# A hybrid decoder layer: the mixer in two passes over the tokens, with thirty gather batches of the channel mixer inside the second

## What is computed

```
h  = RMSNorm(x) * (1 + scale1) + shift1
y  = sigmoid(h @ W_gate_a) * (o_mla @ W_mla) + sigmoid(h @ W_gate_b) * (o_dil @ W_dilb)
x += gate1 * (y @ W_out)                       # the mixer's end
h2 = RMSNorm(x) * (1 + scale2) + shift2
# channel mixer (PEER): 8 heads, each picks 16 of 16384 experts
q  = h2 @ w_pq ; s = q . sub_keys              # 8 heads x 2 halves x 128 scores
top 16 of each half -> 256 sums -> top 16 pairs -> eidx, g = softmax
a  = gelu(h2 . expert_u[eidx]) * g
x += gate2 * sum over 8 x 16 picks of a * expert_v[eidx]
```

## Time and profile before

| | us |
|---|---|
| median of 3 runs | 4351.54 |
| lowest and highest | 4319.0, 4370.52 |
| the profiled execution's own time | 4370.86 |
| its span | 4369.1 |
| TensorE busy | 3802.1 (87%) |
| VectorE busy | 2723.7 (62%) |
| ScalarE busy | 1199.4 (27%) |

### The profile page before, as it was taken

How to read it: one execution, slowest core, us unless ns; L and a number is a source line. 1 busy time by engine, 2 the same in 40 slices (tenths; PEclk the granted TensorE clock), 3 DMA queues, 4 the chain that set the end, 5 groups by cost and what they waited for, 6 DMA issues and landing times.

```text
span 4369.1 us, 43255 instructions
## 1 busy us (share of the span) xinstructions
PE 3802.1 (87%) x14474; PEld 2490.1 (57%) x14474; DVE 2723.7 (62%) x6374; ACT 1199.4 (27%) x3244; POOL 859.8 (20%) x718
## 2 busy tenths in 40 slices
PE   8798899999981899967997677799999999899896
PEld 7575377888970788953453444344454444445443
DVE  2764562533534111258999987767779676967876
ACT  2564432322332111122222567421111111111111
POOL 0000000001000000003333223333333333344332
PEclk8898998995985899988999888899999999999997
DMA  4001102203116111237888879999999999999997
GB/s 158 7 1 42 29 37 80 81 20 119 51 40 208 55 41 36 100 108 282 323 327 318 314 302 376 399 417 409 410 399 378 414 412 387 384 409 412 387 354 279
DMA packets 255851, 1016.29 MB, mean 233 GB/s; under 512 B 28650, under 2 KB 103810, under 8 KB 170642
## 3 DMA queue, kind: packets, MB, share of 16 engines
q0 software_dynamic: 101520, 723.10, 41.9%
q1 hardware_dynamic: 131218, 280.65, 17.4%
q10 hardware_dynamic: 22896, 9.80, 0.8%
HBM read 964.22 MB, written 49.25 MB: 232 GB/s over the span
## 4 chain that ended last, share of the span: by engine, by line
PE 27%; DVE 15%; DMA 11%; issue 2%; ACT 2%; SPq 0%; POOL 0%; ACTq 0%; DVEq 0%
PE banks L2488 9%; PE banks L2474 9%; DMA ff_room<-in_v 7%; PE banks L2463 4%; DVE ff_rows L2137 4%; PE banks L2411 2%; DVE ff_acc L2103 2%; DMA gates_dram<-ff_room 2%; PE banks L2356 1%; DMA ff_rows<-in_uv,pk_expert 1%; DVE pk_eq L1793 1%; DVE pk_axes L1798 1%; DVE mx_x L2163 1%; PE banks L2435 1%; DVE pk_besti L1772 1%
## 5 line engine op out<-in xcount | busy, mean ns | idle before, releaser
L2035 POOL DMA_INDIRECT ff_rows<-in_uv,pk_expert x640 | 803.0, 1255 | 1519.2 <-DVE ff_acc L2103 831.8
L2137 DVE CUSTOM_DVE_ANT_0 ff_rows<-ff_rows,ff_h_row 128x1024 f32<-128x1024 f32 x648 | 766.6, 1220 | 45.3 <-DMA ff_rows<-in_uv,pk_expert 43.4
L2488 PE MATMUL banks<-ff_room,mx_x 128*128 128x512 f32 x1536 | 702.3, 608 | 57.9 <-DVE mx_x L2178 31.2
L2474 PE MATMUL banks<-mx_x,ff_room 128*128 128x384 f32 x2048 | 685.7, 488 | 12.2 <-ACT mx_x L2321 12.2
L2463 PE MATMUL banks<-ff_rows,o_mla_tops 128*128 128x512 f32 x904 | 446.5, 643 | 144.5 <-ACT o_mla_tops L2231 140.8
L2474 PEld LDWEIGHTS banks<-mx_x,ff_room 128*128 128x128 f32 x2048 | 390.3, 191 | 313.0 <-issue 77.3
L2488 PEld LDWEIGHTS banks<-ff_room,mx_x 128*128 128x128 f32 x1536 | 297.3, 195 | 418.9 <-issue 357.8
L2103 DVE SCALAR_TENSOR_TENSOR ff_acc<-ff_rows,ff_a,ff_acc 128x1024 f32<-128x1024 f32 x388 | 498.6, 1285 | 7.2
L2463 PEld LDWEIGHTS banks<-ff_rows,o_mla_tops 128*128 128x128 f32 x904 | 179.1, 206 | 361.8 <-issue 198.5
L177 PE MATMUL banks<-d_w_high,h_high 128*128 128x512 f32 (+1 forms) x648 | 274.3, 423 | 21.9 <-DVE d_w_low L184 21.0
L2219 ACT ACTIVATE ff_gelu<-ff_dots 128x2 f32<-128x2 f32 x324 | 65.7, 203 | 824.9 <-DVE ff_dots L2137 824.7
(11 more groups left out here) (391 smaller groups left out, 5660.3 us busy)
## 6 DMA issues: line engine op xcount, KB each, us to landing
ff_room<-in_uT SPq DMA_DIRECT2D x128, 512.0 KB, 14.4
ff_room<-in_v SPq DMA_DIRECT2D x128, 512.0 KB, 20.6
gates_dram<-ff_room SPq DMA_DIRECT2D x6, 4096.0 KB, 16.8
mx_x<-gates_dram SPq DMA_DIRECT2D x128, 192.0 KB, 17.2
d_w<-in_w_dil POOLq DMA_DIRECT2D x9, 2048.0 KB, 8.3
d_w<-in_w_ada POOLq DMA_DIRECT2D x32, 512.0 KB, 4.7
ff_room<-in_w_pq SPq DMA_DIRECT2D x32, 512.0 KB, 4.5
ff_rows<-in_uv,pk_expert POOLq DMA_INDIRECT x640, 10.8
```

The source lines that it names most:

```text
L2035: pool.indirect_dma_start(out=rows[r][:, :], out_offset=None, in_=IN["uv"][:, :], in_offset=bass.IndirectOffsetOnAxis(ap=at, axis=0))\
L2137: ins = dve.tensor_tensor_reduce(rows[r][:, 0:D], rows[r][:, 0:D], h_row[i % 2][:], 1.0, 0.0, ALU.mult, ALU.add, dots[:, B % RB, j:j + 1])
L2474: ins = pe.matmul(SD[:, 0:ND], u[e % 4][:, k, :], hd[:, k, :], start=(k == 0), stop=(k == KD - 1))
L2488: ins = pe.matmul(Y[j][:, half], ad[e % 2][:, j * P:(j + 1) * P], v[e % 4][:, half_rows[half]], start=(e == 0), stop=(e == NK - 1))
```

## The change

The mixer goes over the tokens in two passes: tokens 0 to 255 (the first two tiles) as one column block of 256, gates, output projection and normalisation, and then tokens 256 to 1031 in two blocks of 388. A unit is now one gate with its branch for one block: 16 units in pass 1, 32 in pass 2 (`z` counts them). Weights are loaded once for each pass, one block of 512 KB at a time, in four slots in pass 1 and two in pass 2. The two slots that pass 2 leaves are the ring of two batches (`RB` = 2 in `stage_mix`).

Behind unit 1 of pass 2 (`ROUTER_AT`) stand the router of tiles 0 and 1 and the picks of the first half of tile 0's heads; the rest of tile 0's picks behind units 2 to 4. Then 30 of tile 0's 64 batches (`MIX_BATCHES`) stand behind the units of `BATCH_AT`; the six last ones lie in the output projection. All their sums are VectorE's, into `acc0`. The sums of a batch stand in front of the mixer products of the next unit.

The channel mixer begins with batch 30 of tile 0 as its batch `B` = 0 and has 98 in place of 128 before the dense loop. It has no router in front; the rows of `h` go out through SP's queue, between the weight loads of the late router, from two buffers that are free at the time. VectorE's early sums are now at every third of batches 3 to 30. The tables `PIECES`, `HOT0` (58 for 61) and `HOTS` (three quads a batch for two) are set anew.

```diff
+EARLY, MIX_BATCHES = 2, 30
 def stage_mix(c):
+    CB = (TOK - NE) // 2
+    PASSES = [[(0, NE)], [(NE, NE + CB), (NE + CB, TOK)]]
+    SUBS = [(p, m, side, i) for p in range(2) for m in range(KD) for side in range(2) for i in range(len(PASSES[p]))]
+    NB, RB = MIX_BATCHES, 2
+    ROUTER_AT = 1
+    BATCH_AT = [z for z in range(5, 31) if z not in (16, 28)] + list(range(33, 48, 2))
+    batch_at = {z: b for b, z in enumerate(BATCH_AT[0:NB])}
...
+            @block.gpsimd
+            def _(pool):
+                pool.wait_ge(s["half_tile"], 1)
+                for b in range(NB):
+                    for j in range(G):
+                        r = b % RB * G + j
+                        if b >= RB:
+                            pool.wait_ge(s["rsum"], (b - RB) * G + j + 1)
...
+                def gated(u):
+                    p, m, side, i = SUBS[u]
+                    if u >= 3:
+                        pe.wait_ge(s["y"], u - 2)
+                    for k in range(KO):
+                        pe.matmul(out, wb[b % 2][:, side * KO + k, :], src[:, k, c0:c1], start=(k == 0), stop=(k == KO - 1))
+                    pe.wait_ge(s["w_lo"], n + 1)
+                    for k in range(KD):
+                        ins = product3(pe, gate, w_parts(n, k), [t[:, k, c0:c1] for t in h_parts], k == 0, k == KD - 1)
...
+                def weights(b):
+                    act.wait_ge(s["dot"], b + 1)
+                    act.activation(act_of[:, b % RB], dots[:, b % RB], ACT.Gelu).then_inc(s["gelu"], 1)
+                    act.wait_ge(s["gelu"], b + 1)
+                    for j in range(G):
+                        ins = act.activation(a[:, b % RB, j:j + 1], act_of[:, b % RB, j:j + 1], ACT.Copy,
+                                             scale=c.gate0[:, b * G + j:b * G + j + 1])
+                    ins.then_inc(s["a"], 1)
...
+                def sums_due(z):
+                    if z in batch_at and batch_at[z]:
+                        sums(batch_at[z] - 1)
...
+                for z in range(len(SUBS) - S1):
+                    sums_due(z)
+                    mixed(S1 + z)
+                    for n in made_after(S1 + z):
+                        w_low(dve, n)
+                    if z == ROUTER_AT:
+                        for hp in range(HP):
+                            dve.wait_ge(s["sc_copy"], hp + 1)
+                            for part in range(4):
+                                top16(part, hp)
+                                dve.wait_ge(s["top"], hp * 4 + part + 1)
+                        pk.prepare(dve)
+                        picks(0)
+                        picks(1)
+                    if 2 <= z <= 4:
+                        picks(z)
+                    dots_due(z)
...
 def stage_ffn(c):
-    batches = [(i, b) for i in range(NS) for b in range(TAILB if i == TAIL else PER)]
+    batches = [(i, b) for i in range(NS) for b in range(0 if i else MIX_BATCHES, TAILB if i == TAIL else PER)]
-    PICK0, HOT0, HOTS = HP * LATE_PER + 3, HP * LATE_PER + 13, 2
+    PICK0, HOT0, HOTS = HP * LATE_PER + 3, HP * LATE_PER + 10, 3
-    TURN0 = 112
+    TURN0 = 86
-    PIECES = {4 + 8 * k: (1, k) for k in range(5)}
-    PIECES |= {PICK0 + 10 * j + 2 * k: (t, k) for j, t in enumerate(DENSE) for k in range(5)}
-    PIECES |= {PICK0 + 59 + 3 * k: (2, k) for k in range(5)}
+    PIECES = {2 + 6 * k: (1, k) for k in range(5)}
+    PIECES |= {PICK0 + at + step * k: (t, k) for t, at, step in zip(DENSE, (0, 6, 16), (1, 2, 2)) for k in range(5)}
+    PIECES |= {PICK0 + 29 + 3 * k: (2, k) for k in range(5)}
-    ON_VEC = list(range(LATE_PER, HP * LATE_PER, LATE_PER))
+    ON_VEC = list(range(LATE_PER, first[1] - 1, LATE_PER))
+    transit = [acc[1], h_row[1]]
...
-                for n in range(2 * HP):
+                for n in range(HP):
                     if n >= 2:
                         sp.wait_ge(s["q_mm"], n - 1)
+                    sp.dma_start(w[n % 2], IN["w_pq"][n]).then_inc(w_in[n % 2], 16)
+                    if n == 1:
+                        for i in range(2, NS):
+                            t0, m = TILES[SPARSE[i]]
+                            sp.wait_ge(s["h_copy"], i)
+                            sp.dma_start(c.dram["h_rows"][t0:t0 + m], transit[i % 2][0:m]).then_inc(h_out[i % 2], 16)
...
-                for hp in range(HP):
-                    dve.wait_ge(s["sc_copy"], hp + 1)
-                    for part in range(4):
-                        top16(dve, part, range(EARLY), hp)
-                        dve.wait_ge(s["top"], hp * 4 + part + 1)
```

More of the change, by code:

```diff
@@ L1563, in stage_mix @@
         ts = sb("ts", [P, KD, NSA])
[L1564 to L1568 removed]
+        dots, act_of, a = (sb(t, [P, RB, G]) for t in ("dots", "gelu", "a"))
@@ new lines, in _ @@
+                for n in range(S1, S1 + 4):
+                    weight(n)
+                sp.wait_ge(s["mm"], S1)
+                residual(0)
+                for n in range(S1 + 4, W1):
+                    weight(n)
+                branch(KD)
+                branch(KD + 1)
+                weight(W1)
+                weight(W1 + 1)
+                keep(0)
+                weight(W1 + 2)
+                for n in range(2, HP):
+                    queries(n)
+                weight(W1 + 3)
@@ new lines, in sums @@
+                def sums(b):
+                    dve.wait_ge(s["a"], b + 1)
+                    for j in range(G):
+                        v, weight = ring[:, b % RB * G + j, D:2 * D], a[:, b % RB, j:j + 1]
+                        if b == 0 and j == 0:
+                            ins = dve.tensor_scalar(acc, v, weight, None, ALU.mult)
+                        else:
+                            dve.wait_ge(s["rsum"], b * G + j)
+                            ins = dve.scalar_tensor_tensor(out=acc, in0=v, scalar=weight, in1=acc, op0=ALU.mult, op1=ALU.add)
+                        ins.then_inc(s["rsum"], 1)
```

658 lines of the change are left out of this document (428 added, 230 removed).

## The result

| | before | changed |
|---|---|---|
| median of 16 runs, us | 4364.77 | 4306.22 |
| lowest and highest | 4319.0, 4373.51 | 4296.85, 4322.61 |
| profiled span | 4369.1 | 4300.1 |

The account below looks back on a forecast made before the run. TensorE bounds the mixer, VectorE then mostly the channel mixer, DMA its last stretch and the dense loop. Mixer +87 and channel mixer -155 give -68: 4303 profiled, 4351.5 - 68 = 4284 us timed, range 4222 to 4365.

Parts of the forecast that it names:

- thirty units of pass 2: Mixer behind the router: TensorE needs 205 us, VectorE's path sums to 214, plus a little mutual loss: 218.
- channel mixer to batch 4: Start of the channel mixer to batch 4's dots: 143 us before, router's 77 gone, 58 expected, bounds 45 and 70.
- Prices: Mixer unit costs: split product 0.120 us at 256 columns, 0.176 at 388; pass 2 unit 6.83; VectorE's step 7.2.
- The turn: Switch from pass 2's units to its output projection, put at 3.5 us within that output's 84.
- The 343 us of one-hot rows: Channel mixer batches 58 to 90: VectorE's 305, some 30 of stalls, 8 for ScalarE; bounds 305 and 395.
- The last eight batches: Channel mixer batches 90 to 98: DMA-bound at 418 GB/s, 57 us less what is fetched ahead: 52, bounds 42 and 60.
- The 13 us by which 218 exceeds 205: Pass 2 of the mixer: the only cost claimed for VectorE's 155 us of gathered work.
- Rival 1: Gathers bind in the mixer's two-batch ring: +45 us; with the split product's upper bound 4350, no change; chance 0.17.
- Rival 2: Larger gain: ScalarE's waits fall beside picks (-30), channel mixer's start 45 us (-13), shorter gelu wait: 4235; chance 0.15.
- Rival 3: Slower: TensorE waits for VectorE in pass 2, so its granted clock falls; in-between case 4410; chance 0.11.
- The signs: Expected profile: pass 2 VectorE gaps over 1 us only before sums, TensorE idle 0.4 us a unit, dense loop 1418 us.
- The drain: Skill's 1.38 us beside each ScalarE table load; by it sigmoid comes 0.5 us behind the sums, sum 12 us larger.

Follow-up runs that it names:

- without the stores: Changed kernel with the gates' HBM table filled from expert_v, so ScalarE does not wait for the five stores: total 2826.7 us, ratio 0.9744.
- pieces at the stalls: Changed kernel with sixteen mixer batches, rows of h stored by GpSimd, and pieces of picks placed where VectorE stalled: 2845.9 us, ratio 0.9812; again 2844.0, 0.9823.

## Why the prediction was right, and where it was not

The sign held, and every stage moved the way that was said; which work paid was in part another than the prediction says (below, "What bounds"). Term by term, from the mixer's first matmul:

| term | predicted | measured |
|---|---|---|
| pass 1 with its output | 108 | 114.2 |
| first two units, router | 14 + 77 | 13.7 + 74.6 |
| thirty units of pass 2 | 218 | 222.5 |
| output of pass 2, with the turn | 84 | 90.3 |
| tail | 15 | 15.6 |
| **mixer** | 516 | 531.0 |
| channel mixer to batch 4 | 58 | 54.4 |
| to 48, 58 | 327, 77 | 320.9, 83.0 |
| to 90, 98 | 343, 52 | 345.7, 44.0 |
| **channel mixer** | 857 | 848.0 |

By these terms the change is -62, not -68: 15 too little in the mixer and 9 too much in the channel mixer. That the spans differ by -69.0 all the same is in part luck. The stages ahead gave 3.7 us and the idle time in front of the first matmul 5.0, neither of which had a price, and the end cost 2.0.

- **Prices.** The split product was taken at 0.120 us and measured 0.118, a unit of pass 2 at 6.83 and measured 6.85, VectorE's step at 7.2 and measured 7.27, its wait for the weights at 0.85 and measured 0.78. The slope from 256 to 344 columns carried over to both new widths.
- **The mixer's 15 us.** Pass 1 is 6 longer, since its first unit waits 2.5 for a weight split and then runs at half the clock (granted clock 0.50; 0.21 us a split product up to 1451, then 0.118). The turn was put at 3.5 us and took 7.5: "two engines so near to each other lose a little to one another" was right, but the place was not. The prediction looked for 0.4 us of idle TensorE a unit; from 1692 to 1835 there is none. Beside it 8.2 us of TensorE's wait up to 1684.8 stand behind the picks. A cost that the prediction left out comes behind each of these two waits: from 1685 to 1690 and from 1872.6 to 1876 the granted clock was 0.50, the lower level, and some 18 split products took 0.32 us in place of 0.176, some 2.6 us each time. The thirty units took 221 to 222 us in the runs with two, sixteen and twenty batches as well, so most of their excess over TensorE's 205 is not the batches' doing. Against that, the first matmul comes 5 us nearer to the stage ahead (an idle time of 4.4 for 9.4 us), probably as the first loads are smaller.
- **Channel mixer.** The first late query came 29.0 us behind its start (30 to 35 predicted). The 343 us of one-hot rows, called the weakest term, were 345.7, and for the reason given: 305 of VectorE's work (303) and 38 of stalls and ScalarE (39). The split of those 38 into 30 and 8 was wrong: without the stores 6 us beside VectorE's work are left. The last eight batches were priced at the rate of a full DMA (418 GB/s); they ran at 352 and a share of 0.88 and moved some 15.5 MB, so more was fetched ahead of them than was reckoned.
- **What bounds.** "From 1878 on the channel mixer is bound by VectorE" is the step that misleads, though the sum carried the right numbers. The largest gain beside the router's move, 67 us, came from the last stretch of the earlier trace rows, which the same paragraph called DMA-bound and the sum priced by gathers (111 to 52; measured 111 to 44). The prediction spoke of VectorE's 155 us moved under TensorE; the runs with two, sixteen and thirty batches show that what paid was gathers taken out of a full DMA stretch, and that once that stretch was gone a batch moved, with the closer tables that it needs, cost more than it brought. The 13 us by which 218 exceeds 205 were called the price of VectorE's gathered work; by the runs with fewer batches twenty cost next to nothing and thirty 6 to 10 us, most of it at the end of the mixer.
- **Rival 1**, gathers that bind in the ring of two: no. Its reason "for" (VectorE has no slack) held, its reason "against" (DMA nearly idle) did not, since the gathers themselves bring DMA to 0.88. They landed in 8.2 us (median, 1690 to 1940), and VectorE waited 7.1 us for them in all. **Rival 2**: no; batch 4 came after 54.4 us and not 45, and 40 us of VectorE's waits were left in the one-hot rows. **Rival 3**: the granted clock was 1.00, full speed, from 1692 to 1865, and 0.85 in the 50 us of the picks. What it describes did happen, but only for the few microseconds behind TensorE's two long waits.
- **The signs.** From 1693 to 1870 us VectorE had gaps of over 1 us outside of the place named: three of 2.6 us for a sigmoid, and two for gathers (1.3 and 1.9). The dense loop, from the first to the last matmul of its first kind (L2474), took 1421.0 us for 1418.2.
- **The drain.** The 0.5 us and 12 us that the prediction works out for it are low by its own terms: 2.65 + 1.38 us is 0.6 behind the 3.4, 14 us over 23 units. It changes nothing in the sum.
- **From the trace to the median.** The 4284 us are 22 under the measured 4306. -68 was right for the pair of profiles; the base was not. The three runs shown had a median of 4351.5, sixteen have 4364.8, and from that the same sum gives 4297. The "19.3 us under the profiled execution" were a low draw, not a property of the kernel.

## What to carry to other kernels

In this kernel, work that was moved into a stage with room paid by what bound the place it left, which may be another resource than the one that it fills in its new place: read the stretch that loses it, and price the second half of what is moved apart from the first. Where two engines hand work back and forth a few units deep, a small loss of the slower one (0.4 us a unit here) shows nearly all at once, at the next full hand-over; a larger one (sums behind the products) uses up the lead and shows as gaps, nine there. An instruction order that looks late (sums in front of the products) may be what hides another engine's table load; count what stands ahead of the awaited instruction in the other engine's row.

## What was not expected of the hardware

The stages ahead of the mixer, whose code is the same in all kernels here, end between 1400.1 and 1455.4 us, and twice the same kernel (pieces at the stalls) at 1433.9 and 1455.4. These two spans differ by 19.6 us, and what lies behind the stages by 1.9 the other way. The stretch from 800 to 1200 us, in the run with sums behind products (end at 1405.9) and, in the second fence, in the changed kernel (1435.5):

```profile
800.00:1200.00 400.00, 371.33 (x1780) 341.00 (x1780) 176.76 (x509) 126.38 (x303) 16.94 (x21) 0.95 0.20 66
```

```profile
800.00:1200.00 400.00, 375.38 (x1641) 349.35 (x1642) 164.62 (x474) 117.76 (x283) 16.90 (x21) 0.85 0.19 63
```

At a granted clock of 0.95 for 0.85 TensorE gets through 1780 matmuls in place of 1641 in the same 400 us. The run without the wait for the stores, which has the earliest end of all (1400.1), is at 0.95 there too; the twelve others are at 0.83 to 0.86. What makes the clock differ between executions stays open. For a reader it means that spans of single profiles are to be compared from a common point behind such stages.
